# A rewritten opening: two tiles turned by products with diag(rstd), the norm weight in the evictions, filler products

## The reference

```
h   = concat(meta_tokens, x)                     # 16 + 512 rows
u   = h * rsqrt(mean(h*h) + 1e-6) * norm_g       # RMSNorm, per row
proj = u @ w_in                                  # 1024 -> 10 x 1024
...  # branch A: gated linear recurrence; branch B: differential attention
m   = sigmoid(ga) * yA + sigmoid(gb) * yB
out = rmsnorm(h + m @ w_out, final_g)            # the 512 rows of x
```

## Time and profile before

| | us |
|---|---|
| median of 3 runs | 755.91 |
| lowest, highest | 755.86, 756.56 |
| the profiled execution, its own time | 756.83 |
| its span, first to last instruction | 755.0 |
| PE busy | 734.7 (97%) |
| DVE busy | 452.3 (60%) |
| ACT busy | 282.7 (37%) |
| GpSimd busy | 23.0 (3%) |
| mean granted TensorE clock of the core | 0.993 of full |

### The profile page before, as it was taken

One profiled execution on the slowest core, in us unless ns is written; L12 is line 12 of the kernel. 1 busy time (PEld: TensorE's weight loads), 2 busy tenths in 40 slices (PEclk: granted clock), 3 DMA queues, 4 the chain that ended last, 5 costly groups with the idle time before them and its releaser, 6 DMA issues.

```text
span 755.0 us, 12973 instructions
## 1 busy us (share of the span) xinstructions
PE 734.7 (97%) x4665; PEld 653.8 (87%) x4665; DVE 452.3 (60%) x1019; ACT 282.7 (37%) x548; POOL 23.0 (3%) x34
## 2 busy tenths in 40 slices
PE   2999999999999999999999999999999999999996
PEld 2998999999899899989989989998888888888885
DVE  4567669558667856955876685695643333233342
ACT  5414443542552444264155235426423222232232
POOL 2000000000000000000000000000000000000000
PEclk9899999999999999999999999999999999999998
DMA  7421220230132122023012212302323233323602
GB/s 264 124 73 56 86 83 13 70 111 28 56 91 76 56 83 83 0 83 111 28 56 83 83 48 85 90 0 85 112 85 112 87 90 102 111 84 95 238 29 112
DMA packets 105416, 63.44 MB, mean 84 GB/s; under 512 B 2066, under 2 KB 100772, under 8 KB 105396
## 3 DMA queue, kind: packets, MB, share of 16 engines
q1 hardware_dynamic: 105076, 62.52, 27.4%
q10 hardware_dynamic: 320, 0.66, 0.3%
HBM read 61.07 MB, written 2.10 MB: 84 GB/s over the span
## 4 chain that ended last, share of the span: by engine, by line
PE 96%; SPq 1%; issue 1%; DMA 1%; DVE 0%; ACT 0%; POOLq 0%; POOL 0%; DVEq 0%; ACTq 0%
PE ps L381 26%; PE ps L382 26%; PE ps L383 26%; PE ps L502 3%; PE ps L571 3%; PE ps L597 2%; PE ps L488 1%; PE ps L588 1%; PE ps L598 1%; PE ps L536 1%; PE ps L535 1%; PE ps L518 1%; PE ps L543 1%; DMA rows_in<-in_da_norm_g 1%; PE ps L527 1%
## 5 line engine op out<-in xcount | busy, mean ns | idle before, releaser
L381 PE MATMUL ps<-uT_hi,w_hi 128*128 128x512 f32 (+3 forms) x960 | 324.7, 338 | 0.0
L382 PE MATMUL ps<-uT_lo,w_hi 128*128 128x512 f32 (+3 forms) x960 | 308.7, 322 | 0.0
L383 PE MATMUL ps<-uT_hi,w_lo 128*128 128x512 f32 (+3 forms) x960 | 308.3, 321 | 0.0
L381 PEld LDWEIGHTS ps<-uT_hi,w_hi 128*128 128x128 f32 x960 | 181.9, 190 | 16.3 <-issue 2.1
L383 PEld LDWEIGHTS ps<-uT_hi,w_lo 128*128 128x128 f32 x960 | 181.2, 189 | 13.9
L382 PEld LDWEIGHTS ps<-uT_lo,w_hi 128*128 128x128 f32 x960 | 181.9, 189 | 11.1
L252 DVE TENSOR_TENSOR w_lo<-w_raw,w_hi 128x1024 fp32r<-128x1024 f32 x104 | 127.0, 1221 | 96.2 <-ACT w_hi L247 95.2
L247 ACT ACTIVATE w_hi<-w_raw 128x1024 fp32r<-128x1024 f32 x104 | 109.4, 1052 | 87.5 <-PE ps L383 84.2
L803 ACT ACTIVATE e<-e,small 128x144 f32<-128x144 f32 (+3 forms) x64 | 36.3, 569 | 71.4 <-DVE small L1195 70.8
L1128 DVE TENSOR_REDUCE small<-sq 128x4 f32<-128x512 f32 x16 | 11.0, 686 | 44.8 <-ACT sq L795 44.8
L371 POOL TENSOR_TENSOR small<-small 128x4 f32<-128x4 f32 x16 | 16.1, 1009 | 510.5 <-DVE small L1130 363.6
(11 more groups left out here) (185 smaller groups left out, 983.1 us busy)
## 6 DMA issues: line engine op xcount, KB each, us to landing
w_raw<-in_w_in SPq DMA_DIRECT2D x80, 512.0 KB, 3.7
w_raw<-in_w_branch_a SPq DMA_DIRECT2D x8, 512.0 KB, 3.5
w_raw<-in_w_branch_b SPq DMA_DIRECT2D x8, 512.0 KB, 3.6
w_raw<-in_w_out SPq DMA_DIRECT2D x8, 512.0 KB, 3.8
x_in<-in_x SPq DMA_DIRECT2D x4, 512.0 KB, 7.7
x_res<-in_x SPq DMA_DIRECT2D x4, 512.0 KB, 6.6
out<-y_out SPq DMA_DIRECT2D x8, 256.0 KB, 2.3
rope<-in_c_rope SPq DMA_DIRECT2D x1, 528.0 KB, 6.2
```

Source lines behind the costliest of these rows:

```text
L381: pe.matmul(dst, w[0], rhs[0], start=start, stop=False, skip_group_check=True)
L382: pe.matmul(dst, w[0], rhs[1], start=False, stop=False, skip_group_check=True)
L383: return pe.matmul(dst, w[1], rhs[0], start=False, stop=stop, skip_group_check=True)
```

## The change

The order of the tiles for mean and power becomes meta, 0, 1, 2, 3. Meta is squared on DVE; norm_g is loaded for 16 partitions only, GpSimd multiplies meta by it before the powers, and by rstd after the third power. Tiles 0 and 1 are no longer multiplied: DVE makes diag(rstd) from the identity for each, and PE forms x^T diag(rstd) as an ordinary fp32 product, eight per tile. Tiles 2 and 3 are multiplied by rstd alone and turned by transposes as before. The norm weight, loaded as 8 rows of 128 and turned to a column per feature tile (g_col), is applied in the evictions out of PSUM, as a scale on ACT and a factor on DVE; these are now 128x256, a feature tile of a pair of token tiles. PE runs 12 products on a tile of zeros at the start and 8 more after meta's turn. The first half section comes ahead of tile 2's turn, and the turn of rows_in comes after `half_section(1, 0)`. ACT issues meta, the rows of norm_g, the identity, and norm_g for 16 partitions, in this order.

```diff
-X_ORDER = (0, 1, CH, 2, 3)
+X_ORDER = (CH, 0, 1, 2, 3)
+WARM = 12
...
+            pool.memset(zeros, 0.0).then_inc(zeros_ready, 1)
             pool.memset(half_neg, -0.5).then_inc(g_pre, 1)
...
+            pool.wait_ge(norm_in, 16)
+            pool.wait_ge(meta_in, 16)
+            pool.tensor_tensor(g_in[:, :], x_in[0:META, CH, :], g_in[:, :], ALU.mult).then_inc(g_pre, 1)
+            pool.wait_ge(g_pre, 6)
             for n, i in enumerate(X_ORDER):
...
+                if n == 2:
+                    pool.wait_ge(x_rstd, 1)
+                    pool.tensor_scalar(g_in[:, :], g_in[:, :], rstd[0:META, CH:CH + 1], None, ALU.mult) \
+                        .then_inc(x_normed, 1)
...
+            def turned(k, i):
+
+                return ps[:, 4 + k // 2, (k % 2) * HALF + (i % 2) * P:(k % 2) * HALF + (i % 2 + 1) * P]
+
+            def scale_and_turn(i):
+                pe.wait_ge(diag_ready, i + 1)
+                for k in range(KT):
+                    mm = pe.matmul(turned(k, i), x_in[:, i, k * P:(k + 1) * P], diag[:, i, :], start=True, stop=True)
+                    if i == 1 and k % 2 == 1:
+                        mm.then_inc(x_turned, 1)
+
+            def turn_x(i):
+                pe.wait_ge(x_normed, i)
+                for k in range(KT):
+                    if i == 2:
+                        pe.wait_ge(u_ready_lo, k // 2 + 1)
+                    t = pe.transpose(turned(k, i), x_in[:, i, k * P:(k + 1) * P], ident[:, :])
+                    if i == 3 and k % 2 == 1:
+                        t.then_inc(x_turned, 1)
...
+            pe.wait_ge(zeros_ready, 1)
+            for _ in range(WARM):
+                pe.matmul(bank(2)[:, P:2 * P], zeros, zeros, start=True, stop=True)
             pe.wait_ge(ident_in, 16)
-            turn_x(0)
-            turn_x(1)
+            pe.wait_ge(g_loaded, 16)
+            pe.transpose(bank(2)[:, 0:KT], g_rows, ident[0:KT, 0:KT]).then_inc(g_turned, 1)
+            scale_and_turn(0)
+            scale_and_turn(1)
+            turn_meta()
+            for _ in range(WARM - 4):
+                pe.matmul(bank(2)[:, P:2 * P], zeros, zeros, start=True, stop=True)
+            half_section(0, 0)
+            turn_x(2)
+            turn_x(3)
+            half_section(1, 0)
             pe.wait_ge(rows_ready, 48)
             pe.transpose(bank(3)[:, 256:256 + 2 * HEADS + 2], rows_in[:, :], ident[0:2 * HEADS + 2, 0:2 * HEADS + 2]) \
                 .then_inc(pe_pre, 1)
-            turn_x(2)
-            turn_x(3)
-            half_section(0, 0)
-            turn_x(4)
-            half_section(1, 0)
             half_section(0, 1)
             half_section(1, 1)
...
+            act.dma_start(x_in[0:META, CH, :], meta_tokens).then_inc(meta_in, 16)
+            act.dma_start(g_rows, norm_g.rearrange("l (k p) -> (l k) p", p=P)).then_inc(g_loaded, 16)
             act.dma_start(ident[:, :], c_ident).then_inc(ident_in, 16)
-            act.dma_start(g_in[:, :], norm_g.to_broadcast([P, D])).then_inc(norm_in, 16)
-            act.dma_start(x_in[0:META, CH, :], meta_tokens).then_inc(meta_in, 16)
+            act.dma_start(g_in[:, :], norm_g.to_broadcast([META, D])).then_inc(norm_in, 16)
...
             square_x(0)
             square_x(1)
+            convert_hi(act, 0, 0, 1)
+            act.wait_ge(g_ready, 1)
+            turned_hi(0)
+            meta_turned_hi()
             square_x(2)
             square_x(3)
             convert_hi(act, 1, 1, 1)
+            turned_hi(1)
...
+            dve.wait_ge(meta_in, 16)
+            meta_x = x_in[0:META, CH, :]
+            dve.scalar_tensor_tensor(meta_sq[:, :], meta_x, 1.0, meta_x, ALU.mult, ALU.mult,
+                                     accum_out=ss[0:META, CH:CH + 1]).then_inc(meta_squared, 1)
             mean_x(0)
+            dve.wait_ge(ident_in, 16)
             mean_x(1)
+            diagonal(0)
+            dve.wait_ge(g_turned, 1)
+            dve.tensor_copy(g_col, bank(2)[:, 0:KT]).then_inc(g_ready, 1)
             mean_x(2)
+            diagonal(1)
+            convert_lo(dve, 0, 0)
+            dve.wait_ge(g_ready, 1)
+            turned_lo(0)
+            dve.wait_ge(meta_hi, 1)
+            dve.tensor_tensor(uT_lo[:, :, 0:META], bank(3)[:, 0:KT * META].rearrange("p (k t) -> p k t", k=KT),
+                              uT_hi[:, :, 0:META].bitcast(F32), ALU.subtract).then_inc(meta_lo, 1)
+            mean_x(3)
+            norm_x(2)
+            mean_x(4)
+            norm_x(3)
+            convert_lo(dve, 1, 1)
+            turned_lo(1)
             dve.wait_ge(pe_pre, 1)
             pre(dve.tensor_copy(lbt, bank(3)[:, 256:256 + 2 * HEADS + 2]))
```

More of the change, by code:

```diff
@@ L151, in build @@
     gate_b, o = at("gate_b", [P, SEQ], F32, o)
+    diag, zeros, g_rows = st[:, 0:2, :], on[:, 0, :], og[0:KT, 0:P]
     kT, o = at("kT", [P, TOK], F32, o)
@@ L712, in _, with square_x @@
             act.sem_inc(gate_taken, 4)
[L714 to L727, removed]
-                                   ACT.Copy).then_inc(u_ready_hi, 1)
-                    return
-                for g in range(2):
-                    ins = act.activation(uT_hi[:, 4 * g:4 * g + 4, META + i * P:META + (i + 1) * P],
-                                         bank(4 + 2 * (i % 2) + g).rearrange("p (k t) -> p k t", k=4), ACT.Copy)
-                ins.then_inc(u_ready_hi, 1)
+            def square_x(i):
+                act.wait_ge(x_loaded[i], 16)
+                if i > 0:
+                    act.wait_ge(x_squared, i)
+                act.activation(x_sq[:, :], x_in[:, i, :], ACT.Square, accum_out=ss[:, i:i + 1]).then_inc(x_squared, 1)
@@ new lines, in meta_turned_hi, with turned_hi @@
+            def meta_turned_hi():
+                act.wait_ge(meta_turned, 1)
+                act.activation(uT_hi[:, :, 0:META], bank(3)[:, 0:KT * META].rearrange("p (k t) -> p k t", k=KT),
+                               ACT.Copy).then_inc(meta_hi, 1)
+            def turned_hi(half):
+                for j in range(KT // 2):
+                    act.wait_ge(x_turned, KT // 2 * half + j + 1)
+                    for k in (2 * j, 2 * j + 1):
+                        ins = act.activation(uT_hi[:, k, META + half * HALF:META + (half + 1) * HALF],
+                                             ps[:, 4 + j, k % 2 * HALF:(k % 2 + 1) * HALF], ACT.Copy,
+                                             scale=g_col[:, k:k + 1])
+                    ins.then_inc(u_ready_hi, 1)
@@ new lines, in norm_x, with turned_lo @@
+            def norm_x(i):
+                dve.wait_ge(x_rstd, i + 2)
+                dve.tensor_scalar(x_in[:, i, :], x_in[:, i, :], rstd[:, i:i + 1], None, ALU.mult) \
+                    .then_inc(x_normed, 1)
+            def turned_lo(half):
+                for j in range(KT // 2):
+                    dve.wait_ge(u_ready_hi, KT // 2 * half + j + 1)
+                    for k in (2 * j, 2 * j + 1):
+                        lo, hi = (a[:, k, META + half * HALF:META + (half + 1) * HALF] for a in (uT_lo, uT_hi))
+                        ins = dve.scalar_tensor_tensor(lo, ps[:, 4 + j, k % 2 * HALF:(k % 2 + 1) * HALF],
+                                                       g_col[:, k:k + 1], hi.bitcast(F32), ALU.mult, ALU.subtract)
+                    ins.then_inc(u_ready_lo, 1)
```

79 lines of the change are left out of this document (19 added, 60 removed).

## The result

| | kernel before | changed kernel |
|---|---|---|
| median, 8 runs each | 756.47 | 758.57 |
| lowest to highest | 755.86 to 757.17 | 757.88 to 758.99 |
| profiled execution, own time (span) | 756.83 (755.0) | 758.99 (757.1) |
| scaling or turning of tile 0 starts | 9.89 | 13.41 |
| first product | 19.47 | 22.38 |

The ratio is 1.0027, 95% interval 1.0018 to 1.0036: the changed kernel is 0.27% slower, 2.1 us in the medians. I had forecast 753.7, in a range of 751.4 to 755.8. The measured time lies outside it: I forecast a gain of 2.2 and the kernel lost 2.1. The profiled execution of the changed kernel was the slowest of its eight, 0.4 above their median; that of the kernel before was 0.4 above its own.

The account below looks back on a forecast made before the run. PE was taken to bound the kernel, so its opening counts one for one. First product earlier -1.6, clock -2.0, tile 2's turn +0.95, waits and rows turn +0.5: total -2.15, giving 753.7, range 751.4 to 755.8.

Parts of the forecast that it names:

- What bounds the kernel: Whole span: PE never waits after the first product, so the opening's gain or loss reaches the end one for one.
- mark: Start of section 2 on PE, the point measured by: 33.81 in the kernel before, forecast at 31.65.
- Transfers: Opening loads: norm_g shrinks from 512 KB to 64 KB; issued fourth by ACT, it lands at about 5.5.
- t0: When PE can begin to scale and turn tile 0: forecast 9.55, against 9.89 in the kernel before.
- first eviction to first product: Evictions by ACT and DVE, then meta's remainder: first product 3.8 after the first pair, at 17.85.
- first product to mark: PE's products, turns of tiles 2 and 3 and short waits up to section 2: 13.8.
- The held port: Opening: GpSimd's scaling of meta (1.8) may hold up DVE's convert_lo(0): 1 us in W, nothing in the forecast.
- -2.0: First 24 products: second fillers keep PE dense, so they run at full clock, saving 2.0 us.
- P: Rival: GpSimd's multiplication takes 4.8 or norm_g lands at 8; mark 33.85, 755.9, no change; chance 0.15.
- W: Rival: clock stays up over PE's idle stretch before t0; mark 29.4 to 30.4, 751.5 to 752.5; chance 0.28.
- N: Rival: clock not raised before the first product, scaling 7.2, second fillers at half rate; mark 36.7, 758.8; chance 0.08.
- Z: Rival: opening is shorter, but a later conversion makes PE wait for it; no change; chance 0.07.

Follow-up runs that it names:

- f1: Changed kernel with norm_g for 16 partitions issued by SP ahead of x tile 0, no longer by ACT; median 753.58, ratio 0.9958 to the kernel before.
- a2: Changed kernel with ACT issuing norm_g for 16 partitions first and the identity last; median 756.63, ratio 1.0 to the kernel before.
- c2: Changed kernel with GpSimd multiplying meta by itself, not waiting for norm_g (meta rows not the reference's); median 754.04, ratio 0.9968 to the kernel before.
- a1: Changed kernel with GpSimd's multiplication of meta by norm_g, and its waits, moved behind the third power; median 755.05, ratio 0.9985 to the kernel before.
- a3: Changed kernel without both batches of filler products; median 760.01, ratio 1.0046 to the kernel before.
- h2: d1 without the second batch, the 8 filler products behind meta's turn; median 753.83, ratio 0.9967 to the kernel before.
- d2: d1 with 16 and not 12 filler products in the first batch; median 752.49, ratio 0.9948 to the kernel before.
- e1: d1 with tiles 0 and 1 multiplied by rstd on DVE and turned by transposes, not products with diag(rstd); median 753.96, ratio 0.9966 to the kernel before.
- d1: Changed kernel with meta's multiplication on DVE instead of GpSimd, x tile 0 first, identity issued first by ACT; median 752.55, ratio 0.9945 to the kernel before.
- a4: a1 with the identity issued first by ACT; median 755.02, ratio 0.9986 to the kernel before.
- b1: Kernel before with filler products alone: 5 after tile 1's turn, 7 after meta's turn; median 755.7, ratio 0.9987 to the kernel before.
- h1_no_first: d1 without the first batch of 12 filler products; median 753.25, ratio 0.9956 to the kernel before.

## Why the prediction was wrong

**What bounds the kernel.** Right. PE has no wait from the mark on, in any of these kernels; section 2 came 2.92 later, the last product 2.79 later. "One for one" to the end of the span is off by 0.7, see what stays open.

**The step that failed** is in *Transfers*: "the small norm_g is fourth ... and lands at about 5.5 (bounds: 3.9, as x0, and 8.5, by norm_g's 6.8)". It landed at 9.4, outside the bounds. The same paragraph had the identity at 5.7; it landed at 8.0. I took size for what counts. f1 and a2 show that place counts: the same 64 KB take 2.4 issued first on SP, 3.3 first on ACT, 7.2 fourth on ACT. First place also means an issue at 0.74 and not at 2.19, ahead of most of SP's loads; no run separates place from moment. That the wait for it is the loss is shown by f1 (5.46 at the mark and 5.0 in the median with this issue alone moved) and c2 (5.7 and 4.5). f1's mark, 31.27, and median, 753.58, are close to the forecast's 31.65 and 753.7, though not term by term: its scaling began 1.1 earlier than forecast, and the evictions and the wait behind them took that back. A row of the kernel before, in the same view as the earlier trace rows, said as much, and I took no price from it:

```profile
x_in<-in_meta_tokens ACTq DMA_DIRECT2D x1, 64.0 KB, 6.9
```

Its 64 KB, third on ACT, took 6.9. They stood behind the 512 KB of norm_g, so this row alone does not tell place from bytes ahead, but it was the nearest price for a small transfer late in ACT's order.

The forecast of 31.65 was off by 5.08, term by term:

| term | forecast | measured | off |
|---|---|---|---|
| norm_g ready, GpSimd starts | 5.5 | 9.55 | +4.05 |
| to the start of scaling (t0) | 4.05 | 3.86 | -0.19 |
| t0 to the first eviction | 4.5 | 4.44 | -0.06 |
| first eviction to first product | 3.8 | 4.53 | +0.73 |
| first product to mark | 13.8 | 14.35 | +0.55 |

Two of the signs that I had named came: GpSimd's start was off by more than a microsecond, and PE waited for more than 0.5 between the first product and section 2. The third, a clock up at t0, did not.

**GpSimd's multiplication.** 2.34 against my 2.6. The instruction itself was never the trouble. The estimate of 2.25 made from the Trainium skill (GPSIMD Engine Reference, section 3.1) was nearer, and the trace agrees with it.

**The held port.** I had convert_lo(0) held up by the scaling of meta. What was held is diagonal(1), a one-input DVE instruction:

```profile
14.11 2.84 POOL L382 TENSOR_SCALAR g_in<-g_in,small 16x1024 f32<-16x1024 f32 x1
14.16 1.13 DVE L998 TENSOR_SCALAR st<-ident,small 128x128 f32<-128x128 f32 x1 [0.67 <-POOL small L378]
15.21 1.21 DVE L258 TENSOR_TENSOR w_lo<-w_raw,w_hi 128x1024 fp32r<-128x1024 f32 x1
```

1.13 and not 0.28, and 2.37 in a1, while convert_lo(0) kept its 1.21. GpSimd's scaling of meta, which I had at 1.8 with bounds of 1.1 and 3.3, took 2.84 here and 3.84 in a1, where convert_lo(0) began 0.08 ahead of it; no run has it undisturbed. The exclusive lock of the Trainium skill (SBUF — State Buffer, section SBUF: two separate sides) fits a1, where DVE ends with POOL's instruction; here DVE ended 1.66 before it, which the lock for the whole instruction does not describe. Nor does that lock describe convert_lo(0): it reads two tiles in SBUF and would have waited for the end of GpSimd's instruction at 16.95, but ran from 15.21. None of it was on the path of the changed kernel: diagonal(1) ended at 15.3, PE needed it at about 17.

**Scale and turn, the clock.** Right in size: half clock from t0, back 3.9 later (I had 4.5), first eviction 4.44 after t0, clock up at the first product. So -2.0 was earned: its 24 products took 3.1, against 4.97. a3 and h2 show what the second batch is worth: from the first product to the mark 15.70 and 15.84 without it, 14.35 with it, so about 1.4 and not 2, since without it the clock is lost only for part of the half section. At the mark it is 1.0 to 1.1, because their first products came 0.3 and 0.5 sooner, for reasons of their own executions.

**Evictions** were under-priced. DVE follows ACT by 0.96 and not by 0.7, and its eight take 3.23, 0.40 apart, against 2.75 (0.35 apart); these two are the +0.73. The same 3.23 made the one wait between S and the mark, 0.58 ahead of the third half section; I had expected those evictions to be in time. Tile 2's and 3's norms took 0.75 each and not 1.1, which cost nothing and gained nothing.

**Rivals.** P was the right one by mechanism ("everything waits on it, and the small norm_g is last in ACT's order"), at 0.15, and mis-sized: it stopped at a landing of 8 and at no change, 755.9. Its "Against: eight times fewer bytes" is what the changed kernel itself refutes: 7.2 against 6.8. W did not come in the changed kernel; h2 and d2 show that it is possible. N did not come either: the clock was back at 17.3, 3.9 after t0. But its numbers, mark 36.7 and 758.8, are those measured, 36.73 and 758.57. That is coincidence: N has them from fillers and products at half clock behind a t0 of 9.55, the run from a t0 of 13.41 with both at full clock. A reader who compared the numbers alone would have taken N. N's mechanism is seen in e1, where it makes up 1.5 of the 2.0. Z did not come.

**What stays open.** Why a small transfer is so slow beside the big ones. The Trainium skill (DMA: Bandwidth & Descriptors, section Queues, rings and completion order) has each DMA engine take turns between queues by whole packets of many descriptors, which would make each small transfer in ACT's queue wait its turn behind SP's packets. The traces fit in that landings get later along ACT's order (changed kernel: meta first at 4.2, identity third at 8.0, norm_g fourth at 9.4), and that even the 4 KB of d1 took 5.93. The step is not a fixed price: from first to second place it was 0.6 in a4 and 2.4 in a2, with 0.45 of issue in each. No run here took SP's loads away, so the mechanism is not shown. Open too: from the start of the last product to the end of the span the changed kernel and its variants need 6.7, the kernel before and b1 7.4. The engines' work there takes as long in both; the 0.7 lies behind the issue of the last store (3.1 to the end of the span against 3.8). It is why the median rose by 2.1 and the mark by 2.9, and it is part of what every variant gains on the kernel before, though it is not in the opening: 0.7 of d1's 4.0.

## What to carry to other kernels

Price a transfer by its place among all that is issued in the same microseconds, and not by its bytes alone (here 64 KB took 2.4 to 7.4, and 512 KB second on ACT 6.8); an instruction that waits for the last small one must not stand in an in-order queue ahead of what everyone needs. Issue first what is waited for first, and check that the reordering does not only move the lateness to the next in line, as in a2 and a4. Filler products pay where they bridge the last wait ahead of dense work and end before it does; where the clock is down already, they stand in the way at twice their length, as in e1 and b1 (b1 still gained 0.64 at the mark by the clock behind them).

## What the runs showed of the hardware

- The column of the granted clock reads 1.00 in all these traces from the start of the span until its first change, and is no evidence there. In h1_no_first:

```profile
8.00:10.00 2.00, 2.00 (x11) 2.00 (x10) 0.93 (x7) 0.73 (x1) 1.06 (x2) 1.00 1.06 386
...
12.00:14.00 2.00, 2.00 (x21) 1.85 (x21) 1.42 (x4) 2.00 (x6) 0.00 (x0) 1.00 1.14 370
```

  11 records in two microseconds against 21 at the same reading. The distance of the records from each other is what tells the clock.
- An fp32 product of 128x128 by 128 columns is two records and takes some 0.23 at full clock (2.05 for eight, latency included), 0.45 at half (5.49 for the first twelve fillers). A transpose of the same size is one record and takes half of that: 1.09 for eight at full clock in e1, 1.97 at half in the earlier trace rows.
- Transposes too were followed by a full clock. In b1 PE did nothing but 16 transposes from 9.98 to 13.3 (3.48 in all), and the ten filler records right behind them took 1.28, 0.12 apart.
- DVE multiplies 128x1024 fp32 by a column in 0.75 (tensor_scalar, SBUF to SBUF) and 128x128 in 0.28 to 0.29. A line through the two, an estimate, gives 0.22 for every instruction and 0.53 more for 1024 columns; that makes 0.49 for 528 columns, near the 0.553 of the earlier trace rows. I had 1.1 by doubling the 0.553, which counts the fixed part twice.
- GpSimd multiplies two 16x1024 fp32 tiles in 2.34, and in 3.27 (a2) and 3.28 (f1) where DVE's square of meta began just ahead of it; meta by itself, beside the same square, took 2.85 (c2).
